# Every second row's mean of squares by statistics operations on VectorE, in a planned decoder-layer kernel on eight cores

## Chip, cores, metric
One Trainium2 chip, 8 cores, one launch. Every core computes 2048 of the 16384 positions. The time is the device time of the slowest core in microseconds (us). The engines are TensorE (PE), VectorE (DVE), ScalarE (ACT), GpSimd (POOL) and SyncE (SP).

## What is computed
One decoder layer, float32 in and out, width 1024. Cut to what matters here:

```
h = rms_norm(x, g_pre_mix)            # x / sqrt(mean(x*x) + 1e-6) * g, over the 1024 columns
proj = h @ w_in                       # q, k, v (768 each), pool input 256, gates 2048
q, k = rope(q), rope(k)
# attention in three head groups: (window, dilation) = (128,1), (512,4), (2048,16)
# multi-scale pooling branch, gated merge, output projection, norm, residual
x = x + rms_norm(merged @ w_out, g_post_mix)
gu = rms_norm(x, g_pre_ffn) @ w_gate_up
x = x + rms_norm((silu(a) * b) @ w_down, g_post_ffn)
```

The change is in the first `rms_norm` alone.

## The kernel before
A core reads its own 2048 rows (xo) and the 2048 rows ahead of them (xh, the halo, which the long attention windows need), each as 16 row blocks of 128 x 1024 float32. In the loop at line 896, 32 turns, blocks are taken in pairs. Both blocks of a pair get a sum of squares: the first (e = 0) by ScalarE's Square with an accumulator (L907), the second (e = 1) by a scalar_tensor_tensor of VectorE that multiplies the block with itself and accumulates (L905). ScalarE makes both into 1/sqrt with an Ln and an Exp over two columns (L909, L910). Then `to_feature_major` lets ScalarE copy the block, scaled, to bfloat16 (xsb, a ring of two), TensorE transpose it in eight pieces against ident, and VectorE copy the result from PSUM into hT (own rows) or hTh (halo). x blocks have eight buffers (xst), halo blocks five (xsth).

From hT and hTh come first the projections of the dilation-16 group: q2 and k2 per 512 rows (`qk2_unit`, through `rope`: two groups of eight 512-wide matmuls, four multiplications with the rotary table tab on VectorE into rt, a ring of two, and two additions on GpSimd), and v2 in 16 blocks per half (`v2_unit`, eight 256-wide matmuls each), every one of which reads all 16 row blocks of its half. The weights wq2, wk2, wv2 are loaded by GpSimd's queue and multiplied with the gains on VectorE (`gained`). Then the other two groups' projections (wq01, wk01, wv01), dilation-16 attention, and per 512 rows attention, pooling and merge; then output projection and the feed-forward part.

The order of the work isn't written out. The program records all operations as nodes; `schedule` simulates the five engines with the costs of `op_cost`, the priority of a node being its number plus a bias per part (table `PART`, L26), and what comes out is each engine's fixed order. Where TensorE would idle over 1 us in the simulation, `fill` (L356) puts matmuls on a constant tile warmw there. VectorE operations with two inputs in SBUF of more than one column and GpSimd operations exclude each other in the simulation (`port`, L153). Loads at the start wait for the load five before them (`behind`, FLIGHT); `WV_AT` (L24) says after how many x blocks the load of wv2 stands. Most operations bear line L522 or L524 in the profile, a helper's lines; tiles tell them apart.

Of the kernel before, what the change touches and what calls it, by code (L numbers as in the profile page):

```python
# [6 lines left out]
F32 = mybir.dt.float32  # L7
BF16 = mybir.dt.bfloat16
AF = mybir.ActivationFunctionType
ALU = mybir.AluOpType  # L10
# [3 lines left out]
D = 1024  # L14
# [4 lines left out]
EPS = 1e-6  # L19
# [1 line left out]

MERGE_AT = 1
FLIGHT = 5
WV_AT = 10  # L24

PART = {"norm": -615, "norm_h": -320, "qk2": 0, "k2h": -175, "v2": 650, "v2h": 15, "f-1": 90, "f0": 40, "f1": 0, "f2": 40, "f3": 0, "g2": -435,  # L26
        "a0": -100, "a1": 295, "a2": 0, "a3": -25, "p0": 0, "p1": 0, "p2": -15, "p3": 135, "m01": 0, "m23": 0, "w01": 0, "gv2": 275, "wg": 25}
ARENA_BASE = 18432
ARENA_BYTES = 229376 - ARENA_BASE

# [176 lines left out]
def peek(a):  # L207
    return a.resolve(0) if isinstance(a, View) else a


def in_psum(a):
    return type(peek(a).tensor).__name__.startswith("PSum")


def nelem(ap):
    n = 1
    for _, c in list(ap.ap)[1:]:
        n *= int(c)
    return n
# [6 lines left out]
def unit_step(ap):  # L226
    d = [x for x in list(ap.ap)[1:] if int(x[1]) > 1]
    return not d or int(d[-1][0]) in (0, 1)
# [5 lines left out]
def op_cost(eng, method, aps, kw):  # L234
    n = nelem(peek(aps[0]))
    if eng == "tensor":
        if method == "transpose":
            return 0.06
        rows = int(list(peek(aps[1]).ap)[0][1])
        return 0.013 + 0.00025 * n if rows <= 64 else max(n * 0.000422, 0.03)  # L240
    strided = not all(unit_step(peek(a)) for a in aps[1:])
    if eng == "scalar":
        n = max(n, nelem(peek(aps[1])))
        return 0.19 + 0.00086 * n + (0.19 if "accum_out" in kw else 0.0)
    if eng == "vector":
        if method == "reciprocal" or kw.get("op") == ALU.divide:
            return 0.1 + 0.00645 * n
        if all(peek(a).dtype == BF16 and not in_psum(a) for a in aps):
            return 0.12 + 0.00060 * n
        if method == "tensor_copy" and all(peek(a).dtype == BF16 for a in aps):  # L250
            return 0.14 + 0.00054 * n
        return 0.12 + 0.00110 * n
    if kw.get("op") == ALU.pow:
        return 0.55
    if method == "tensor_scalar":
        return 0.2 + 0.0026 * n
    return 0.17 + (0.0040 if strided else 0.0021 if unit_step(peek(aps[0])) else 0.0025) * n
# [316 lines left out]
def build_program():  # L574
# [30 lines left out]
    P = Prog(nc)  # L605
    pe, act, dve, pool, sp = P.pe, P.act, P.dve, P.pool, P.sp
# [14 lines left out]
    o = 0  # L621

    def take(nbytes):
        nonlocal o
        r = o
        o += (nbytes + 63) // 64 * 64
        return r


# [10 lines left out]
    nhalf = P.sb("nhalf", [128, 1], F32, take(4))  # L640
    uh = P.sb("uh", [128, 2, 16], F32, take(128))
    st = P.ring("st", [128, 2], F32, [take(8) for _ in range(16)], False)
    st4 = P.ring("st4", [128, 4], F32, [take(16) for _ in range(3)], False)
    R_HT = take(32 * KB)
    R1 = take(32 * KB)
# [15 lines left out]
    v2 = P.sb("v2", [128, 16, 2, 6, 64], BF16, R2 + 24 * KB)  # L661
# [7 lines left out]
    junk = P.ring("junk", [128, D], BF16, [R3 + 32 * KB + i * 2 * KB for i in range(2)], False)  # L669
# [32 lines left out]
    def x_load(i):  # L702
        src, ring = (xo, xst) if i < NT else (xh, xsth)
        j = i % NT
        t = ring.new()
        t.tok = sp.dma(t[:, :], src[j * 128:(j + 1) * 128, :], after=behind())
        loads.append(t.tok)
        sp_x.append(t.tok)
        return t
# [31 lines left out]
    def w2_load(w, src, got, todo, c, name):  # L741
        got.append(pool.dma(w[:, c, :, :], src[4 + c], dsem(name), after=behind()))
        loads.append(got[-1])
        todo.append((w[:, c, :, :], got[-1]))
# [5 lines left out]
    for c in range(2):  # L750
        w2_load(wk2, wk_d, d_wk2, g_wk2, c, "d_wk2_%d" % c)
    xt += [x_load(i) for i in range(4, WV_AT)]
    d_wv2 = pool.dma(wv2[:, :, :], wv_d[2], dsem("d_wv2"), after=behind())
    loads.append(d_wv2)
    xt += [x_load(i) for i in range(WV_AT, NT + 5)]

# [103 lines left out]
    gk_k2 = [gained(w, d, 128) for w, d in g_wk2]  # L860
    P.bias = PART["gv2"]
    gk_v2 = gained(wv2[:, :, :], d_wv2, 256)
# [33 lines left out]
    for i in range(2 * NT):  # L896
        halo = i >= NT
        P.bias = PART["norm_h" if halo else "norm"]
        if i % 2 == 0:
            pair = [xt.pop(0), xt.pop(0)]  # L900
            sums, sqs = st4.new(), []
            for e, u in enumerate(pair):
                src, j_ = u[:, :], junk.new()
                if e == 1:
                    sqs.append(dve.scalar_tensor_tensor(out=j_[:, :], in0=src, scalar=1.0, in1=src, op0=ALU.mult, op1=ALU.mult, accum_out=sums[:, e:e + 1], after=[u.tok]))  # L905
                else:
                    sqs.append(act.activation(out=j_[:, :], in_=src, func=AF.Square, accum_out=sums[:, e:e + 1], after=[u.tok]))  # L907
                j_.free(sqs[e])
            ln = act.activation(out=sums[:, 0:2], in_=sums[:, 0:2], func=AF.Ln, scale=1.0, bias=D * EPS, after=sqs)  # L909
            sums.tok = act.activation(out=sums[:, 2:4], in_=sums[:, 0:2], func=AF.Exp, scale=-0.5, after=[ln])  # L910
        t = pair[i % 2]
        j = (i % NT) * 128
        cp, h_ok[i] = to_feature_major(t[:, :], sums, any1, xsb.new(), None, (hTh if halo else hT)[:, :, j:j + 128], [],
                                       x_cp[:NT] if halo else [], col=2 + i % 2)
        t.free(cp)
        x_cp.append(cp)
        if halo and i + 5 < 2 * NT:
            xt.append(x_load(i + 5))
        if i % 4 == 3:
            s = (i // 4) % 4  # L920
            P.bias = PART["k2h" if halo else "qk2"]
            if not halo:
                qk2_unit("q", s, False)
            qk2_unit("k", s, halo)
        if i == NT - 1:
            P.bias = PART["v2"]
            for r in range(16):
                v2_unit(r, False)
            todo = [("k%d" % c, wk01[:, c, :, :], wk_d[c]) for c in range(4)] + [("v%d" % g, wv01[:, g, :, :], wv_d[g]) for g in range(2)]
            todo += [("u%d" % c, wu[:, c, :, :], wu_d[c]) for c in range(2)] + [("q%d" % c, wq01[:, c, :, :], wq_d[c]) for c in range(4)]  # L930
    P.bias = PART["w01"]
    d_masks = sp.dma(masks[:, :, :], masks_d[:, :, :], dsem("d_masks"), after=[sp_x[-1]])
# [4 lines left out]
    for g in range(4):  # L937
        c, hf = g // 2, g % 2
        d_mix.append(pool.dma(wmixb[64 * hf:64 * hf + 64, c, 64 * hf:64 * hf + 64], wmix_d[g, :, :], dsem("d_mix%d" % g), after=[sp_x[-1], m_mix]))
    P.bias = PART["v2h"]  # L940
    for r in range(16):
# [581 lines left out]
```

How the kernel before makes its waits and increments, by code:

```python
    def emit(self):  # L480
# [19 lines left out]
                if e.seen.get(proc, 0) >= val:  # L500
                    continue
                e.seen[proc] = val
                snap = self.procs[proc].snaps.get(val)
                if snap:
                    for k, v in snap.items():
                        if e.seen.get(k, 0) < v:
                            e.seen[k] = v
                s = self.procs[proc].sem
                e.meta.append(("wait", proc, val))
                e.ops.append(lambda q, s=s, val=val: q.wait_ge(s, val))
            sem, step = (sem, 16) if n.dma else (e.proc, 1)
            many = len(n.items) if n.dma else 1
            sem.count += step * many
# [6 lines left out]
                k = {q: res(x) for q, x in kw.items()}  # L520
                if n.dma or j == len(n.items) - 1:
                    e.ops.append(lambda q, m=method, a=a, k=k, s=sem.sem, v=step: getattr(q, m)(*a, **k).then_inc(s, v))
                else:
# [2 lines left out]
    def finish(self, last):  # L526
        e, need = self.sp, {}
        for n in last:
            need[n.tick[0]] = max(need.get(n.tick[0], 0), n.tick[1])
        for p, v in need.items():
            if e.seen.get(p, 0) < v:
                e.meta.append(("wait", p, v))
                e.ops.append(lambda q, s=self.procs[p].sem, v=v: q.wait_ge(s, v))
```

## Time and profile before

| | |
|---|---|
| median of 3 runs | 974.02 us (973.38 to 975.49) |
| profiled execution | 975.52 us, slowest core's span 972.5 us |
| spans of the eight cores | 964.8 to 972.5 us |
| TensorE busy | 937.4 us |
| VectorE busy | 473.3 us |
| ScalarE busy | 342.1 us |
| GpSimd busy | 353.9 us |
| granted TensorE clock, mean of the core | 0.986 |

The span is the time from the slowest core's first to its last instruction; the 3.0 us between it and the execution's own time lie around it. Busy times of engines overlap. A granted clock of 1 is 2.4 GHz.

### The profile page before, as it was taken

Reading aid. Unit: us, or ns where it says so; the run is one execution under the profiler, and the core shown is the slowest. Engines: PE = TensorE matmul, PEld = TensorE weight load, DVE = VectorE, ACT = ScalarE, POOL = GpSimd, SP = SyncE. Lnnn points to the kernel's source line nnn. Section 1 sums busy time; section 2 is a strip of 40 time slices with the busy share of each in tenths; the row PEclk is TensorE's granted clock in tenths of the full one; section 3 lists DMA queues with packets and bytes.
Section 4 is the critical chain, followed back from the end, with each engine's and each line's share of the span. In section 5 each row is a group of like instructions: output and inputs, shape, how many; then the busy total and the mean of one; then the engine's idle time right before and its main releaser. Section 6 shows DMA issues by size and latency. Waiting matters only on the chain.

```text
span 972.5 us, 15020 instructions; the slowest of 8 cores (964.8 to 972.5 us)
## 1 busy us (share of the span) xinstructions
PE 937.4 (96%) x5416; PEld 472.7 (49%) x5416; DVE 473.3 (49%) x560; ACT 342.1 (35%) x555; POOL 353.9 (36%) x334
## 2 busy tenths in 40 slices
PE   8879999989999999999999999999999999999997
PEld 3446776644554454444444444444444444444443
DVE  4889886686887867575454111111223111111323
ACT  4667426553445446434483111110101111110211
POOL 1447855467865584775693101110001000000000
PEclk8899999998999999999999999999999999999999
DMA  8936852451223477554377666563233545350221
GB/s 203 277 120 224 184 112 75 96 149 44 45 66 80 74 151 148 168 133 116 109 240 186 116 125 114 106 111 85 89 130 109 84 68 86 66 87 1 87 109 65
DMA packets 41224, 112.76 MB, mean 116 GB/s; under 512 B 5984, under 2 KB 14688, under 8 KB 41056
## 3 DMA queue, kind: packets, MB, share of 16 engines
q0 software_dynamic: 14432, 45.65, 27.7%
q1 hardware_dynamic: 26320, 66.07, 20.7%
q8 instruction: 44, 0.72, 0.3%
q14 instruction: 28, 0.23, 0.1%
q10 hardware_dynamic: 400, 0.08, 0.0%
HBM read 136.14 MB, written 21.30 MB: 162 GB/s over the span
## 4 chain that ended last, share of the span: by engine, by line
PE 84%; issue 4%; DVE 4%; DMA 3%; POOL 2%; ACT 2%; DVEq 0%; ACTq 0%; POOLq 0%; SPq 0%
PE ps L524 74%; PE ps L522 10%; DMA wq<-wq 1%; DMA wgs<-wg 1%; POOL x1b L522 1%; POOL st L522 1%; DVE junk L522 1%; ACT xsb L522 1%; DVE PT L522 1%; DMA tab<-tab 1%; DVE x1b L522 1%; DVE rt L522 0%; ACT junkd L522 0%; ACT xs L522 0%; DVE val L522 0%
## 5 line engine op out<-in xcount | busy, mean ns | idle before, releaser
L524 PE MATMUL ps<-hT,wgu 128*128 128x512 bf16 x1232 | 294.6, 379 | 0.0
L524 PEld LDWEIGHTS ps<-hT,wgu 128*128 128x128 bf16 x1232 | 120.4, 98 | 144.9
L522 DVE TENSOR_TENSOR ffT<-ps,sa 128x512 bf16<-128x512 f32 x88 | 60.8, 691 | 230.5 <-PE ps L522 226.4
L522 ACT ACTIVATE sa<-ps 128x512 f32<-128x512 f32 x88 | 52.4, 596 | 239.9 <-PE ps L522 239.9
L524 PE MATMUL ps<-wdna,ffT 128*128 128x512 bf16 x512 | 115.7, 379 | 1.0 <-issue 0.5
L522 POOL DMA_DIRECT2D wgu<-wgu x44 | 23.6, 537 | 245.8 <-PE ps L522 226.1
L524 PE MATMUL ps<-hT,wgs 128*128 128x512 bf16 x448 | 108.6, 383 | 3.1 <-ACT tg L522 2.1
L522 POOL TENSOR_TENSOR k<-rt 128x512 bf16<-128x512 f32 (+1 forms) x36 | 80.0, 2229 | 42.7 <-DVE rt L522 42.7
L522 DVE TENSOR_TENSOR rt<-ps,tab 128x512 f32<-128x512 f32 (+1 forms) x120 | 76.1, 669 | 20.2 <-PE ps L522 14.7
L522 ACT ACTIVATE junkd<-ps 128x1024 bf16<-128x1024 f32 (+1 forms) x33 | 32.8, 993 | 147.0 <-PE ps L522 147.0
L524 PEld LDWEIGHTS ps<-wdna,ffT 128*128 128x128 bf16 x512 | 50.0, 98 | 61.8 <-issue 1.9
L522 DVE TENSOR_TENSOR x1b<-ps,gfin 128x1024 f32<-128x1024 f32 (+1 forms) x17 | 19.8, 1162 | 116.4 <-ACT junkd L522 109.3
L524 PEld LDWEIGHTS ps<-hT,wgs 128*128 128x128 bf16 x448 | 43.1, 98 | 56.6 <-issue 8.0
L522 PE MATMUL ps<-hT,wgu 128*128 128x512 bf16 x176 | 66.7, 379 | 0.0
L522 DVE SCALAR_TENSOR_TENSOR tg<-tg,ps 128x512 f32<-128x512 f32 x64 | 43.2, 684 | 44.3 <-ACT tg L522 33.6
L522 DVE TENSOR_TENSOR PT<-PT,masks 128x1024 bf16<-128x1024 bf16 x48 | 54.9, 1148 | 18.4 <-ACT PT L522 18.2
L522 ACT ACTIVATE tg<-ps 128x512 f32<-128x512 f32 x64 | 38.1, 595 | 72.3 <-PE ps L522 72.2
L522 POOL TENSOR_TENSOR q<-rt 128x512 bf16<-128x512 f32 x24 | 49.8, 2084 | 37.7 <-DVE rt L522 37.7
L522 ACT ACTIVATE PT<-ps 128x1024 bf16<-128x1024 f32 x48 | 49.1, 1023 | 31.4 <-PE ps L522 31.2
L522 POOL TENSOR_TENSOR mT<-tg 128x512 bf16<-128x512 f32 x32 | 49.3, 1542 | 27.5 <-DVE tg L522 27.4
L524 PE MATMUL ps<-wout,mT 128*128 128x512 bf16 x224 | 53.6, 379 | 0.6 <-DVE tg L522 0.6
L522 DVE TENSOR_TENSOR wgs<-wgs,gains 128x2048 bf16<-128x2048 bf16 x16 | 44.2, 2766 | 4.6 <-DMA wgs<-wg 4.5
(149 smaller groups left out, 1308.3 us busy)
## 6 DMA issues: line engine op xcount, KB each, us to landing
wgu<-wgu POOLq DMA_DIRECT2D x44, 512.0 KB, 6.2
xst<-xo SPq DMA_DIRECT2D x16, 512.0 KB, 8.3
xsth<-xh SPq DMA_DIRECT2D x16, 512.0 KB, 6.1
wgs<-wg POOLq DMA_DIRECT2D x16, 512.0 KB, 6.0
xin<-xo SPq DMA_DIRECT2D x16, 512.0 KB, 5.9
x1s<-x1b SPq DMA_DIRECT2D x16, 512.0 KB, 4.4
xin<-x1s SPq DMA_DIRECT2D x16, 512.0 KB, 4.3
out<-x1b SPq DMA_DIRECT2D x15, 512.0 KB, 2.9
```

Of the source, the lines that this page charges most:

```text
L522: e.ops.append(lambda q, m=method, a=a, k=k, s=sem.sem, v=step: getattr(q, m)(*a, **k).then_inc(s, v))
L524: e.ops.append(lambda q, m=method, a=a, k=k: getattr(q, m)(*a, **k))
```

## The change
The second block of each pair gets its mean of squares from VectorE's statistics: two bn_stats of 512 columns, one bn_aggr that makes mean and variance of the two, and one scalar_tensor_tensor of one column, mean x mean + variance. The first block's Square is scaled by 1/32, so that both are means, and the Ln multiplies by 1024. VectorE writes no junk tile any more; there is a ring bns of three. `op_cost` knows bn_stats. `WV_AT` goes from 10 to 16, many entries of `PART` change, and `take` rounds to 32 bytes instead of 64.

```diff
-WV_AT = 10
+WV_AT = 16
-PART = {"norm": -615, "norm_h": -320, "qk2": 0, ...
+PART = {"norm": -790, "norm_h": -270, "qk2": -50, ...
...
+        if method == "bn_stats":
+            return 0.12 + 0.00110 * nelem(peek(aps[1]))
...
+    bns = P.ring("bns", [128, 14], F32, [take(56) for _ in range(3)], False)
...
-                src, j_ = u[:, :], junk.new()
+                src = u[:, :]
                 if e == 1:
-                    sqs.append(dve.scalar_tensor_tensor(out=j_[:, :], in0=src, scalar=1.0, in1=src, op0=ALU.mult, op1=ALU.mult, accum_out=sums[:, e:e + 1], after=[u.tok]))
+
+                    bn = bns.new()
+                    b6 = [dve.bn_stats(out=bn[:, 6 * h:6 * h + 6], in_=u[:, 512 * h:512 * h + 512], after=[u.tok]) for h in range(2)]
+                    ag = dve.bn_aggr(out=bn[:, 12:14], in_=bn[:, 0:12], after=b6)
+                    sqs.append(dve.scalar_tensor_tensor(out=sums[:, e:e + 1], in0=bn[:, 12:13], scalar=bn[:, 12:13], in1=bn[:, 13:14], op0=ALU.mult, op1=ALU.add, after=[ag]))
+                    bn.free(sqs[e])
                 else:
-                    sqs.append(act.activation(out=j_[:, :], in_=src, func=AF.Square, accum_out=sums[:, e:e + 1], after=[u.tok]))
-                j_.free(sqs[e])
-            ln = act.activation(out=sums[:, 0:2], in_=sums[:, 0:2], func=AF.Ln, scale=1.0, bias=D * EPS, after=sqs)
+                    j_ = junk.new()
+                    sqs.append(act.activation(out=j_[:, :], in_=src, func=AF.Square, scale=1.0 / 32.0, accum_out=sums[:, e:e + 1], after=[u.tok]))
+                    j_.free(sqs[e])
+            ln = act.activation(out=sums[:, 0:2], in_=sums[:, 0:2], func=AF.Ln, scale=float(D), bias=D * EPS, after=sqs)
```

What the planner makes of it differs in the start of the program; TensorE's order is the same in both from behind the dilation-16 attention on.

TensorE, from the first transposes (ident,xsb) on; warmw are filling matmuls. Before:

```order
L524 MATMUL ps<-ident_43,xsb_58_100 128x128 x7
L522 MATMUL ps<-ident_43,xsb_58_100 128x128
L524 MATMUL ps<-warmw_50 128x512 x8
L522 MATMUL ps<-warmw_50 128x512
L524 MATMUL ps<-ident_43,xsb_57_99 128x128 x7
L522 MATMUL ps<-ident_43,xsb_57_99 128x128
L524 MATMUL ps<-ident_43,xsb_58_100 128x128 x7
L522 MATMUL ps<-ident_43,xsb_58_100 128x128
L524 MATMUL ps<-warmw_50 128x512 x2
L522 MATMUL ps<-warmw_50 128x512
```

Now:

```order
L526 MATMUL ps<-ident_43,xsb_61_103 128x128 x7
L524 MATMUL ps<-ident_43,xsb_61_103 128x128
L526 MATMUL ps<-warmw_50 128x512 x2
L524 MATMUL ps<-warmw_50 128x512
L526 MATMUL ps<-ident_43,xsb_60_102 128x128 x7
L524 MATMUL ps<-ident_43,xsb_60_102 128x128
L526 MATMUL ps<-ident_43,xsb_61_103 128x128 x7
L524 MATMUL ps<-ident_43,xsb_61_103 128x128
L526 MATMUL ps<-terms_106,spread_107 128x512
```

Nine and three fills between these transposes and behind them have become three and none. Over the whole start there are 47 fills ahead of the first transposes and 35 behind before, 55 and 9 now.

TensorE, around the last halo transposes. Before, with v2 of the own half (wv,hT) ahead of them:

```order
L524 MATMUL ps<-wv_56_98,hT_73 128x256 x7
L522 MATMUL ps<-wv_56_98,hT_73 128x256
L524 MATMUL ps<-ident_43,xsb_57_99 128x128 x7
L522 MATMUL ps<-ident_43,xsb_57_99 128x128
L524 MATMUL ps<-ident_43,xsb_58_100 128x128 x7
L522 MATMUL ps<-ident_43,xsb_58_100 128x128
L524 MATMUL ps<-warmw_50 128x512 x2
L522 MATMUL ps<-warmw_50 128x512
L524 MATMUL ps<-hTh_74,wk_55_97 128x512 x7
```

Now:

```order
L526 MATMUL ps<-ident_43,xsb_60_102 128x128 x7
L524 MATMUL ps<-ident_43,xsb_60_102 128x128
L526 MATMUL ps<-ident_43,xsb_61_103 128x128 x7
L524 MATMUL ps<-ident_43,xsb_61_103 128x128
L526 MATMUL ps<-hT_76,wk_58_100 128x512 x7
L524 MATMUL ps<-hT_76,wk_58_100 128x512
L526 MATMUL ps<-hT_76,wk_58_100 128x512 x7
L524 MATMUL ps<-hT_76,wk_58_100 128x512
L526 MATMUL ps<-hTh_77,wk_58_100 128x512 x7
```

Ahead of the last transposes stand, beside fills and transposes, 184 matmuls of 512 columns and 128 of 256 before, 152 and 56 now; the rest has moved behind them.

VectorE, at the product of wv2 with the gains. Before:

```order
L522 SCALAR_TENSOR_TENSOR junk_59_101,st_28_70<-xst_42_84 128x1024
L522 COPY hT_73<-ps 128x8x128 x3
L522 TENSOR_TENSOR rt_70_112<-ps,tab_67_109 128x512 x2
L522 TENSOR_TENSOR wv_56_98<-wv_56_98,gains_46 128x2048
L522 COPY hT_73<-ps 128x8x128
```

Now:

```order
L524 BN_STATS bns_28_70<-xst_51_93 128x6 x2
L524 BN_AGGR bns_28_70<-bns_28_70 128x2
L524 SCALAR_TENSOR_TENSOR st_31_73<-bns_28_70 128x1
L524 TENSOR_TENSOR rt_72_114<-ps,tab_71_113 128x512
L524 TENSOR_TENSOR wv_59_101<-wv_59_101,gains_46 128x2048
L524 COPY hT_76<-ps 128x8x128 x2
```

Eight copies into hT stood ahead of it, now twelve, and the sums of all own rows. On GpSimd's queue the load of wv2 stood ahead of the first two rotary additions, now behind them.

## Rows read from the trace of the kernel before

**Rows 1.** The page: engine totals, then TensorE's granted clock in 40 slices.
```profile
PE 937.4 (96%) x5416; PEld 472.7 (49%) x5416; DVE 473.3 (49%) x560; ACT 342.1 (35%) x555; POOL 353.9 (36%) x334
...
PEclk8899999998999999999999999999999999999999
```

**Rows 2.** Stretches: length, busy PE, PEld, DVE, ACT, POOL, clock, DMA, GB/s.
```profile
13.70:67.70 54.00, 42.33 (x250) 21.50 (x248) 42.88 (x56) 33.85 (x55) 19.27 (x9) 0.84 0.73 203
67.70:111.70 44.00, 43.18 (x355) 30.82 (x355) 38.82 (x59) 32.05 (x60) 34.66 (x21) 1.00 0.66 208
```

**Rows 3.** Waits of TensorE before 120 us: total us, times, longest.
```profile
PE ps L524 <- ACT xsb L522: 5.0, 7, 3.0
```

**Rows 4.** Timeline of VectorE: start, length (us), operation.
```profile
13.72 1.22 DVE L522 SCALAR_TENSOR_TENSOR junk<-xst 128x1024 bf16<-128x1024 f32 x1
...
27.84 1.22 DVE L522 TENSOR_TENSOR wk<-wk,gains 128x1024 bf16<-128x1024 bf16 x1
28.97 1.88 DVE L522 TENSOR_TENSOR rt<-ps,tab 128x512 f32<-128x512 f32 x3
...
37.86 2.28 DVE L522 SCALAR_TENSOR_TENSOR junk<-xst 128x1024 bf16<-128x1024 f32 x1 [0.32 <-DMA xst<-xo]
...
59.18 1.88 DVE L522 COPY hT<-ps 128x1024 bf16<-128x1024 bf16 x3
60.97 1.21 DVE L522 SCALAR_TENSOR_TENSOR junk<-xsth 128x1024 bf16<-128x1024 f32 x1
...
62.12 1.28 DVE L522 TENSOR_TENSOR rt<-ps,tab 128x512 f32<-128x512 f32 x2
...
111.04 0.69 DVE L522 COPY hTh<-ps 128x1024 bf16<-128x1024 bf16 x1
```

**Rows 5.** Groups of VectorE, row sums: busy us, mean ns, idle before.
```profile
L522 DVE SCALAR_TENSOR_TENSOR junk<-xst 128x1024 bf16<-128x1024 f32 x8 | 16.5, 2078 | 1.4 <-DMA xst<-xo 1.4
L522 DVE SCALAR_TENSOR_TENSOR junk<-xsth 128x1024 bf16<-128x1024 f32 x8 | 13.2, 1658 | 0.0
```

**Rows 6.** Waits of VectorE from 13.7 to 111.7 us.
```profile
DVE hT L522 <- PE ps L522: 8.5, 7, 2.6
DVE hTh L522 <- PE ps L522: 3.5, 5, 1.2
```

**Rows 7.** Small operations of the pooling branch and the GpSimd addition beside one.
```profile
221.24 1.40 DVE L522 TENSOR_TENSOR uY<-uY,small 64x16 f32<-64x16 f32 x1
222.74 0.16 DVE L522 TENSOR_TENSOR zT<-uY,ps 64x16 bf16<-64x16 f32 x1
...
220.65 1.95 POOL L522 TENSOR_TENSOR q<-rt 128x512 bf16<-128x512 f32 x1
```

**Rows 8.** Timeline of TensorE.
```profile
16.97 0.91 PE L524 MATMUL ps<-ident,xsb 128*128 128x128 bf16 x7 [3.01 <-ACT xsb L522]
...
18.82 3.62 PE L524 MATMUL ps<-warmw 128*128 128x512 bf16 x8
...
22.66 0.72 PE L524 MATMUL ps<-ident,xsb 128*128 128x128 bf16 x7
...
107.74 0.93 PE L524 MATMUL ps<-wv,hT 128*128 128x256 bf16 x7
...
108.61 0.93 PE L524 MATMUL ps<-wv,hT 128*128 128x256 bf16 x7
...
111.88 1.67 PE L524 MATMUL ps<-hTh,wk 128*128 128x512 bf16 x7 [0.30 <-DVE hTh L522]
...
113.60 0.59 PE L524 MATMUL ps<-hTh,wk 128*128 128x512 bf16 x2
```

**Rows 9.** Timeline of ScalarE: Ln and Exp, then the two scaled copies.
```profile
107.40 0.49 ACT L522 ACTIVATE st<-st 128x2 f32<-128x2 f32 x2
107.99 2.19 ACT L522 ACTIVATE xsb<-xsth,st 128x1024 bf16<-128x1024 f32 x2
```

**Rows 10.** Loads of wv by GpSimd's queue: us to landing, of three.
```profile
DMA to landing us min/median/max: 10.4/15.3/16.9
```

More of the change, by code:

```diff
@@ L23 @@
 FLIGHT = 5
-WV_AT = 10
-PART = {"norm": -615, "norm_h": -320, "qk2": 0, "k2h": -175, "v2": 650, "v2h": 15, "f-1": 90, "f0": 40, "f1": 0, "f2": 40, "f3": 0, "g2": -435,
-        "a0": -100, "a1": 295, "a2": 0, "a3": -25, "p0": 0, "p1": 0, "p2": -15, "p3": 135, "m01": 0, "m23": 0, "w01": 0, "gv2": 275, "wg": 25}
+WV_AT = 16
+PART = {"norm": -790, "norm_h": -270, "qk2": -50, "k2h": -175, "v2": 575, "v2h": 0, "f-1": 0, "f0": 50, "f1": 0, "f2": 40, "f3": 0, "g2": -235,
+        "a0": -300, "a1": 270, "a2": 0, "a3": -25, "p0": 0, "p1": 0, "p2": -15, "p3": 135, "m01": 0, "m23": 10, "w01": -10, "gv2": -200, "wg": 0}
 ARENA_BASE = 18432
@@ L625, in take @@
         r = o
-        o += (nbytes + 63) // 64 * 64
+        o += (nbytes + 31) // 32 * 32
         return r
```

## The prediction, blind

> **What bounds the kernel now.** I read the page first: TensorE is busy for 96% of the span, and its granted clock is below full only at the beginning and in one slice near 210 us [rows 1]. So time can be won only where TensorE idles, runs filling matmuls, or runs at the low clock. The table of stretches shows where that is: from 13.7 to 67.7 us TensorE has a mean clock of 0.84 and gaps of 12 us, from 67.7 to 111.7 us it is nearly full at a clock of 1.00 [rows 2]. The list of waits says for whom it waits before 120 us: above all the normalised rows of ScalarE (xsb) [rows 3]. This is the chain that the change touches: row sums, Ln and Exp, scaled copy, transposes, copy into hT or hTh.
>
> The order of TensorE behind the first 143.7 us of its real work is the same in both programs, so I look only at the start. There, two points count. All own rows must be in hT before v2 of the own half can start, and the last halo rows must be transposed before TensorE can finish the halo.
>
> **VectorE's account before.** From 13.72 us, its first row sum, to 111.7 us, its last hTh copy [rows 4], VectorE has 98.0 us. Three multiplications with the rotary table last 1.88 us and two 1.28, so one takes 0.60 from start to start and ends 0.08 later; three copies take 1.79 up to the next instruction, a row sum 1.15, a weight multiplication of 1024 columns 1.13 [rows 4]. The sixteen row sums last 16.5 and 13.2 us [rows 5], where the shortest is 1.21: 16 x 1.22 = 19.5, so 10.2 us of the 29.7 are stretching, a mean of 0.64 for a row. Less 0.08 us each in which the next instruction has begun, they hold the engine for 28.4 us. With 44 rotary multiplications (26.4), 32 copies (19.2), three weight products of 1024 columns and one of 2048 (3.4 + 2.2) the sum is 79.6, and 18.4 us are idle, most of it for TensorE's transposes: 8.5 + 3.5 [rows 6], and 1.4 for x [rows 5].
>
> **The new row sum.** A bn_stats reads 512 columns, one source, nothing from PSUM; no such instruction is in the trace. Nearest is the rotary multiplication of 512 columns, 0.60 from start to start; the two halves have no wait between them, 1.20. Then a dependent bn_aggr and a dependent one-column product. Nearest to those are the small operations of the pooling branch, 0.16 us, which start 0.10 us after the one before has ended [rows 7]. 1.20 + 0.08 + (0.10 + 0.17) + (0.10 + 0.17) - 0.08 = 1.74, I take 1.75. Bounds: 1.4, if most of a gap is covered by a neighbour (the planner puts copies between the halves), and 2.4, if a statistics operation passes its data at two thirds of that rate. So in itself the new form costs VectorE 0.6 us more for a row, 9.6 us for sixteen.
>
> **The stretching.** The last product still has two inputs in SBUF (mean and variance), like the old one. A product of 64x16 that began at 221.24 us lasted 1.40 us, where its neighbour of the same size took 0.16, and ended at 222.64, when GpSimd's addition of 220.65 + 1.95 ended [rows 7]. So size does not protect: it will wait for a running GpSimd addition. But GpSimd starts when a rotary pair is done, the old sum came right behind such pairs and took the whole 2 us, and now 1.5 us of statistics run first. GpSimd is busy for 54 of these 98 us [rows 2], so at random a product would meet 0.55 x 1.0 us, 8.8 in all; the eight old stretchings less 1.5 us each leave 0.9. I take 4 us. ScalarE's side only gets scale=1/32 and scale=1024 in instructions that are there anyway: nothing. The junk buffer that VectorE no longer writes leaves both to ScalarE; its squares come earlier, which costs nothing, since it idles 20 us before 67.7 [rows 2].
>
> The Trainium skill (VectorE: DVE Perf Modes, The TRN2 errata) gives (N + 151) / 0.96 ns for an fp32 tensor_tensor, 0.69 us at 512. The trace has that as the duration (0.69 for one) but 0.60 as the pitch; with 0.69 for each half, as an estimate, the set would be 0.18 us dearer, 2.9 us over sixteen, and the whole sum 0.2 us slower than before instead of faster.
>
> **The new order.** Four moves count.
> First, fills. Behind the first transposes the old order has 35 filling matmuls, nine of them from 18.82 to 22.66 us, at the low clock of 1.2 GHz, 0.43 each, right ahead of transposes that then started without a wait [rows 8]. The new one has 9. The first block grows from 47 to 55; at 0.216 it ends 1.7 us later than 13.96 (16.97 less 3.01), still ahead of the first transposes at 16.97 [rows 8], which themselves wait 0.4 us more for the longer row sum.
> Second, the load of wv2 goes behind x row 15, on POOL behind two additions. x rows 10 to 15 land earlier, their sums stand earlier on VectorE. Its product with the gains now waits for a load that is issued only when row 11 has landed; loads of wv took 10.4 to 16.9 us [rows 10]. Before, VectorE still had to wait for row 9 at 37.86 [rows 4]; with 1 MB less ahead of it row 11 may land near 39, and wv2 from 49 to 54 us. VectorE is there at 13.7 + 8 sets 14.0 + stretching 2 + 9 rotary multiplications 5.4 + 12 copies 7.2 + products 3.4 + idle 4 = 49.7. So it costs from 0 to 5 us, with the copies of rows 12 and 13 queued behind it. I take 0, since the other two wv loads followed four others in the queue, and make the rest a rival.
> Third, less is asked before the last transposes. TensorE then has done 32 wide and 72 narrow matmuls fewer: 32 x 0.215 + 72 x 0.109 = 14.7 us (eight wide in 1.72 us, eight narrow in 0.87 [rows 8]), and VectorE has 32 rotary multiplications instead of 44 ahead of its last hTh copy, 30 ahead of its last row sum. They stand behind.
> Fourth, the memset of v01 stands ahead of the last two hTh copies, 2.3 us; TensorE has other work there (40 wide matmuls, 8.6 us), so nothing; if that cover were gone it would cost those 2.3.
>
> **The sum.** TensorE takes up the halo's last part at 111.88 us [rows 8]. With 14.7 us less behind it, break-even for that point is 97.2. VectorE's new account up to the last row sum: 16 x 1.75 = 28.0, stretching 4, 30 rotary multiplications 18.0, 28 copies 16.8, products 5.6, together 72.4, from 13.7 to 86.1 plus idle. Then Ln and Exp 0.6, two scaled copies 2.2 [rows 9], transposes 0.5: 89.4 plus idle. Idle: x 1.4 [rows 5] and the first transposes 1.2 stay, the longest wait, 2.6 before [rows 6], falls to about 1 with fewer fills, and 1.5 is left of the rest because TensorE has 27 us of work in 36 instead of 42 in 44. That is 5.1, so 94.5, and 97.2 - 94.5 = **2.7 us faster**. The profiled execution took 975.5, the median is 974.0; from the median 971.3.
>
> **Rivals.**
> A, slower: the one-column product meets a GpSimd addition as often as the long one did. Place: VectorE behind each pair of statistics, with ScalarE's Ln and the row's transposes behind it. At the old mean of 0.64 us that is 10.2 us instead of 4: 97.2 - 100.7, 3.5 us slower, 977.5. It turns the sign above 0.42 us a row. For it: the 1.40 us. Against: what GpSimd waits for is done 1.5 us before. The Trainium skill (SBUF — State Buffer, Who interferes with whom) has the rule that a VectorE instruction with two SBUF inputs contends with a GpSimd instruction that reads SBUF; by that rule, the trace agrees with its 1.40 us.
> B, slower: wv2 lands 5 us after VectorE wants it, the late end above: 97.2 - 99.5, 2.3 slower, 976.3; it turns the sign above 2.7 us.
> C, no change: in the halo half ScalarE is the pace. It is busy 32 of 44 us there [rows 2] and would have to do nearly that in 36; five row buffers refill in 6 us. If this half takes 38.7 us instead of 36, 974.0.
> D, no change: the set costs 2.0 us instead of 1.75, because the halves do not overlap as the rotary multiplications do [rows 4] and the aggregate is dearer than the small operations [rows 7]: 4 us more, 1.3 slower, 975.3. The Trainium skill's formula named above lies near this case; the pitch of 0.60 in the trace speaks against it.
> E, much faster: stretching falls to 0.9 us as in the subtraction above. 3.1 more, 5.8 in all, 968.2.
>
> **Numbers.** Forecast 0.37, E 0.14, C 0.14, D 0.10, A 0.13, B 0.12. A difference of 0.2%, 2 us, is about what a measurement of this kernel can tell. Of the forecast 0.05 falls inside it. Faster 0.32 + 0.14 = 0.46, same 0.05 + 0.14 + 0.10 = 0.29, slower 0.13 + 0.12 = 0.25. The range goes from 1.7 below E, 966.5, to A's centre, 977.5; beyond lie half of A and the tail of E, some 0.12.
>
> **What would show it.** Right: bn_stats near 0.68 long and 0.60 apart, sixteen last products with a median under 0.3 and a sum under 7 us, last transposes before 96 us, clock over 0.9 between 40 and 60 us, GpSimd's additions down from 2.4 to 2.0 us. Wrong: one-column products of 1 to 2 us in most sets, a wait for DMA at wv's product, or TensorE waits between 65 and 95 us of more than 11 us.

## The result, and the profile after

The changed kernel took 997.56 us, median of 4 runs (995.61 to 1000.01); the kernel before took 974.02, 973.38 and 975.49 beside it. The ratio is 1.0238, 95% interval 1.0210 to 1.0265: slower by 2.4%. Forecast were 971.3 us, and a range that ended at 977.5. The ratios, and all medians but this first one, leave out executions in which a die was slower than the other at a lower mean clock, and none of which has a trace: 998.37 us among the four above, 1142.69 us beside it, later 1021.71 us of the changed kernel (mean clocks of 0.926 to 0.944 on cores 0 to 3) and 1137.70 us of the kernel before (0.818 to 0.837 on cores 4 to 7).

The result is made of two things of different kinds, a clock and the schedule, and they have to be taken apart first. The spans of the eight cores do it. View: span and mean granted clock of each core, changed kernel.

```profile
core 0: 994.4 us, clock 0.961
core 1: 991.2 us, clock 0.958
core 2: 994.4 us, clock 0.962
core 3: 994.1 us, clock 0.962
core 4: 972.8 us, clock 0.991
core 5: 977.2 us, clock 0.987
core 6: 998.5 us, clock 0.957
core 7: 998.1 us, clock 0.960
```

Six cores are some 20 us longer than the other two, at a mean clock of 0.96 instead of 0.99. Where that is, the stretches of the slowest core and of a fast one show. View: stretches of core 6, then of core 5: length, busy TensorE and its matmuls, granted clock, share of DMA, GB/s.

```profile
46.00:206.00 160.00, 150.03 (x1183) 0.81 0.49 122
206.00:400.00 194.00, 182.37 (x1215) 0.98 0.48 92
```

```profile
46.00:206.00 160.00, 145.73 (x1361) 0.99 0.55 137
206.00:400.00 194.00, 183.06 (x1139) 0.97 0.44 94
```

For 160 us core 6 has a granted clock of 0.81. That is neither of the two levels of [rows 1] and [rows 2] (1.00, which is 2.4 GHz, and half of it): a third one, 0.8125 in the records. TensorE is busy in it and gets fewer matmuls done. View: groups of TensorE's instructions from 120 to 200 us: busy us, mean ns of one, idle before; core 6, then core 5.

```profile
L526 PE MATMUL ps<-hT,wq 128*128 128x512 bf16 x42 | 12.1, 437 | 0.0
```

```profile
L526 PE MATMUL ps<-hT,wq 128*128 128x512 bf16 x56 | 13.4, 380 | 0.0
```

The same matmul lasts 437 ns instead of 380. The level begins at 46.3 to 48.1 us and ends at 206 to 209 us on cores 0, 1, 2, 3, 6 and 7, with stretches of 3.4 us at half clock in it on four of them, and never comes on 4 and 5. The other three runs have no trace, but their spans and mean clocks (0.96 instead of 0.99) are alike: all eight cores are at 991.8 to 994.0 us, or all but cores 0 and 1 (976.2 and 975.2), or all but 2 and 3 (974.8 and 976.4). So cores are spared in pairs. No trace of the kernel before has the level, though TensorE is as busy there.

The Trainium skill (TensorE: Matmul & The Clock Gate, Part 1) names a limiter of 13/16 of the clock, which comes for a whole die once three of its cores run dense matmuls, and holds as long as the load does. The size agrees with the 0.8125. The rest does not, in the traces: the kernel before is as dense on all eight cores without it (96.6 to 98.7 of 100 us busy, from 100 to 200 us, at a clock of 1.00), here two cores of a die went free, and it ended near 207 us while the load went on (182 of the next 194 us busy).

**Without that clock** the changed kernel is still slower. Cores 4 and 5 above say so, and later runs of the same program on three chips (which chip the first timing had is not recorded), with no 0.81 in their three traces: 981.74 us (8 runs, ratio to before 1.0059, interval 1.0040 to 1.0079), 981.04 and 981.47, and 981.16. So some 6 to 7 us of the 23.5 belong to the change's own schedule (5.7 by the ratio, 7.1 by the medians), and some 16 to 17 to the clock. The rest of this section reads core 5, which had the full clock.

View: core 5, groups of VectorE from 13.7 to 97.9 us, just behind the end of its last row sum: busy us, mean ns, idle before. They answer to [rows 5].

```profile
L524 DVE TENSOR_TENSOR rt<-ps,tab 128x512 f32<-128x512 f32 x31 | 20.2, 682 | 2.9 <-PE ps L524 2.6 <-issue 0.3
L524 DVE COPY hT<-ps 128x1024 bf16<-128x1024 bf16 x16 | 10.6, 685 | 3.7 <-PE ps L524 3.6
L524 DVE BATCH_NORM_STATS2 bns<-xst 128x6 f32<-128x512 f32 x16 | 10.4, 681 | 0.0
L524 DVE BATCH_NORM_STATS2 bns<-xsth 128x6 f32<-128x512 f32 x16 | 10.2, 679 | 0.0
L524 DVE COPY hTh<-ps 128x1024 bf16<-128x1024 bf16 x12 | 7.9, 684 | 2.1 <-PE ps L524 1.9
L524 DVE SCALAR_TENSOR_TENSOR st<-bns 128x1 f32<-128x1 f32 x16 | 7.7, 483 | 1.7
L524 DVE BATCH_NORM_AGGREGATE bns<-bns 128x2 f32<-128x12 f32 x16 | 3.3, 206 | 1.2
```

A bn_stats of 512 columns lasts 0.68 us, an aggregate 0.21. The one-column products last 0.483 in the mean; one instruction's view of them (shortest, median, longest in ns) says why.

```profile
L524 DVE SCALAR_TENSOR_TENSOR st<-bns x16: 219/221/1893, 15.6 to 96.0; 128x1 f32<-128x1 f32 x16
```

Most last 0.22, a few up to 1.89. View: timeline of VectorE, then of GpSimd and of ScalarE, around the last of them.

```profile
93.27 0.68 DVE L524 TENSOR_TENSOR rt<-ps,tab 128x512 f32<-128x512 f32 x1
93.87 1.27 DVE L524 BATCH_NORM_STATS2 bns<-xsth 128x6 f32<-128x512 f32 x2
95.07 0.67 DVE L524 TENSOR_TENSOR rt<-ps,tab 128x512 f32<-128x512 f32 x1
95.66 0.19 DVE L524 BATCH_NORM_AGGREGATE bns<-bns 128x2 f32<-128x12 f32 x1
95.95 1.89 DVE L524 SCALAR_TENSOR_TENSOR st<-bns 128x1 f32<-128x1 f32 x1
97.77 0.68 DVE L524 TENSOR_TENSOR rt<-ps,tab 128x512 f32<-128x512 f32 x1
```

```profile
95.88 1.94 POOL L524 TENSOR_TENSOR k<-rt 128x512 bf16<-128x512 f32 x1 [0.18 <-DVE bns L524]
```

```profile
97.94 0.50 ACT L524 ACTIVATE st<-st 128x2 f32<-128x2 f32 x2 [1.45 <-DVE st L524]
98.58 2.19 ACT L524 ACTIVATE xsb<-xsth,st 128x1024 bf16<-128x1024 f32 x2
```

The product of one column begins at 95.95 and ends at 97.84, when GpSimd's addition (95.88 + 1.94 = 97.82) ends; ScalarE's Ln has waited 1.45 us for it. And behind Ln and the copies the last halo rows wait. View: TensorE from 92.7 us.

```profile
92.71 0.93 PE L526 MATMUL ps<-wv,hT 128*128 128x256 bf16 x7
93.47 0.27 PE L524 MATMUL ps<-wv,hT 128*128 128x256 bf16 x1
95.98 0.55 PE L526 MATMUL ps<-ident,xsb 128*128 128x128 bf16 x7 [2.24 <-DVE bns L524]
...
99.88 0.55 PE L526 MATMUL ps<-ident,xsb 128*128 128x128 bf16 x7 [1.11 <-ACT xsb L524]
100.26 0.22 PE L524 MATMUL ps<-ident,xsb 128*128 128x128 bf16 x1
100.92 0.55 PE L526 MATMUL ps<-ident,xsb 128*128 128x128 bf16 x7 [0.43 <-ACT xsb L524]
101.30 0.22 PE L524 MATMUL ps<-ident,xsb 128*128 128x128 bf16 x1
101.36 1.67 PE L526 MATMUL ps<-hT,wk 128*128 128x512 bf16 x7
```

TensorE is through with the last transposes and goes on at 101.36 us, with a group of the own half (hT,wk) that the new order has put there. Forecast for this point were 94.5, break-even 97.2: 4.2 us late, and the core ends 4.7 us later than the core of [rows 8] (977.2 against 972.5).

### The profile page after: what moved, and what is told of

It reads as the page before. It is cut to its first block, busy times and chain, and to the rows that moved or that the text cites. A ratio compares the mean times of both kernels' runs of the same rounds, so it can differ in the third digit from the quotient of the medians.

```text
span 998.5 us, 15099 instructions; the slowest of 8 cores (972.8 to 998.5 us)
## 1 busy us (share of the span) xinstructions
PE 957.4 (96%) x5398; PEld 483.3 (48%) x5398; DVE 475.1 (48%) x592; ACT 343.3 (34%) x555; POOL 343.2 (34%) x334
## 4 chain that ended last, share of the span: by engine, by line
PE 88%; DVE 4%; issue 3%; DMA 2%; ACT 2%; POOL 1%; DVEq 0%; ACTq 0%; POOLq 0%
PE ps L526 77%; PE ps L524 10%; DMA wgs<-wg 1%; DMA wq<-wq 1%; DVE bns L524 1%; ACT xsb L524 1%; DVE rt L524 1%; DVE st L524 1%; DVE hT L524 0%; POOL st L524 0%; DVE val L524 0%; DVE PT L524 0%; DVE wgs L524 0%; DVE den L524 0%; DVE hTh L524 0%
## 5 line engine op out<-in xcount | busy, mean ns | idle before, releaser
L524 POOL TENSOR_TENSOR k<-rt 128x512 bf16<-128x512 f32 (+1 forms) x36 | 71.8, 2005 | 50.7 <-DVE rt L524 50.6
L524 DVE TENSOR_TENSOR x1b<-ps,gfin 128x1024 f32<-128x1024 f32 (+1 forms) x17 | 19.8, 1162 | 116.4 <-ACT junkd L524 116.4
L524 POOL TENSOR_TENSOR mT<-tg 128x512 bf16<-128x512 f32 x32 | 48.1, 1507 | 29.6 <-DVE tg L524 29.5
L526 PE MATMUL ps<-wv,hT 128*128 128x256 bf16 x336 | 48.8, 293 | 2.0 <-DVE hTh L524 1.7
```

Of the source, the lines that this page charges most:

```text
L524: e.ops.append(lambda q, m=method, a=a, k=k, s=sem.sem, v=step: getattr(q, m)(*a, **k).then_inc(s, v))
L526: e.ops.append(lambda q, m=method, a=a, k=k: getattr(q, m)(*a, **k))
```

## Experiments

An order of instructions is kept exactly in most of these kernels: the planner runs as before, and only then are single instructions exchanged. "L" is the start of the last matmul of the halo transposes (101.30 above), mean over the eight cores of the profiled execution. It is 108.8 us before and 100.6 in the changed kernel (`after_again`). Other executions of the same program gave 101.2 and 101.5, so a difference in L of about 1 us says nothing by itself.

### Is it the order or the operations?

`order_products`: after the planner has run, each set gives way to one product (the edit is shortened here, as are those below).

```diff
-bn_stats(bn[0:6], u[0:512]); bn_stats(bn[6:12], u[512:1024]); bn_aggr(bn[12:14], bn[0:12])
-scalar_tensor_tensor(sums, mean, mean, var, mult, add)
+scalar_tensor_tensor(scratch, u, 1/1024, u, mult, mult, accum_out=sums)
```

> The changed kernel's order of instructions on every engine, instruction for instruction, but each of the 16 sets of statistics operations is again one product of the row with itself (scaled by 1/1024, so that all sums keep the changed kernel's meaning); the whole row is read in one instruction of about 1.2 us instead of a set of about 1.75 us. Theory A (the gap in TensorE's work near 34-37 us and what follows it sets off the granted clock of 0.81, whatever VectorE does): the 0.81 stage of about 160 us appears on most cores, the time is 990 to 1000 us. Theory B (the statistics operations themselves set it off): no core shows 0.81, the time is 973 to 981 us. The 8 us in which the changed kernel's undisturbed cores are later than before would stay under theory 'order' and shrink by 3 or more under theory 'sets'.

Measured: 979.77 and 980.29 us, ratio 1.0059 (1.0039 to 1.0079), L 99.9, no 0.81. Taken alone this speaks for theory B. It was run again beside the changed kernel:

> The changed kernel itself, once more. Four executions of it had the granted clock of 0.81 on six or eight cores for about 160 us from 46 to 48 us on, and took 995.6 to 1000.0 us; the kernel with its order but with products (980 us) and the one with 14 fills (979 us) had none, in a session of their own. Theory A' (what sets 0.81 off is in the changed kernel: its gap and its sets together): 0.81 again, 995 to 1000 us, and again not beside it in the kernel with products. Theory D (0.81 belongs to the chip or the session in which the changed kernel was first timed): no 0.81 here, 975 to 981 us.

> The changed kernel's order with products in place of the statistics sets, once more, beside the changed kernel itself. Theory A': no 0.81, 979 to 981 us, while the changed kernel has it. Theory D: both without it or both with it.

Measured on one chip: changed kernel 981.74 us, 1.0059 (1.0040 to 1.0079), L 100.6, no 0.81 anywhere; with products 978.72, 1.0046 (1.0031 to 1.0061), L 99.2. Neither A nor B is left as a sufficient cause of 0.81: the changed kernel itself does without it. Nor is the wait near 34 us, as this view of it on core 3 of `after_again` shows.

```profile
37.73 0.91 PE L526 MATMUL ps<-ident,xsb 128*128 128x128 bf16 x7 [3.70 <-ACT xsb L524]
```

That is the same wait, as long as in the first timing, and the clock was 1.00 or 0.50 all the way behind it. What the pair shows for the change: with products, too, the order costs 4 to 6 us. The sets seem to cost some 1 to 3 us more in it, but the two intervals overlap. As work on VectorE they cost much more than that: the sixteen products hold it for 23 to 27 us on the eight cores of `order_products` (24.7 to 27.9 busy, less 16 x 0.08), the sets for 33.5 (16 x 1.83 and 4.2 of stretching).

`stats_old_order`: the sets in the order of before.

> The kernel before with its own order on every engine, instruction for instruction, but each of VectorE's 16 products in the first 112 us is a set of two bn_stats, a bn_aggr and a one-column product at the same place. Theory A (the order's gap and fills set off the granted clock of 0.81): no 0.81 stage, and the time is that of before plus or minus what the sets cost: 972 to 980 us. Theory B (statistics operations set it off): 0.81 for about 160 us on most cores, 990 to 1000 us.

Measured: 975.87 us, ratio 1.0020 (1.0009 to 1.0031), L 110.8, no 0.81. The sets alone cost 2 us here (by the ratio), although their one-column products are hardly stretched in this order (median 220 ns, longest 1040, 5.3 us in sum instead of 7.1 to 8.3).

### The fills

`after_with_fills` has 14 filling matmuls ahead of the transposes of row 4; `before_no_fills` is the kernel before with `del fills[1].items[3:]` and `order.remove(fills[3])`.

> The changed kernel with 14 filling matmuls of 512 columns ahead of the transposes of row 4, where TensorE waits 3.7 us for ScalarE near 34 us; nothing else moves. Theory A (TensorE's rest near 34-37 us, which lets the granted clock fall to 0.5 and rise again in one step at the same time on all cores, sets off 0.81): no 0.81 stage, 974 to 982 us. Theory B (statistics operations) and theory C (the denser ScalarE and DMA work at 40 to 60 us): 0.81 stays, 990 to 1000 us.

> The kernel before with the filling matmuls of the changed kernel: 3 instead of 9 ahead of the transposes of row 2, and none instead of 9 ahead of those of row 4; nothing else moves. Theory A (the rest near 34 us): a 0.81 stage appears on some cores, and the time goes to 985 to 1000 us. Theories B and C: no 0.81 stage, 973 to 977 us (the fills only cover a wait).

Measured: with fills 978.53 and 979.57 us, L 99.9; before without them 975.43 us, 1.0015 (1.0005 to 1.0025), L 110.0, no 0.81 in either. So the fills of the kernel before are worth 1.5 us, which my sum had at nothing; and a wait near 36 us (1.65 us on its slowest core, not 3.7) did not bring the low level. As tests of theories A and B all runs of this chip are weak, since the changed kernel itself was not timed there and later did without the level too.

### The form of the last operation

```diff
-scalar_tensor_tensor(out=sums, in0=mean, scalar=mean, in1=var, op0=mult, op1=add)
+tensor_scalar(out=sums, in0=mean, scalar1=mean, scalar2=var, op0=mult, op1=add)
```

> The changed kernel with the one-column product (mean times mean plus variance) written as a tensor_scalar with two scalars read from memory, so that it has one tensor input from SBUF instead of two; nothing else moves. Theory 'GpSimd stretches two-input operations alone': its 16 executions fall from 8.0 us in sum (longest 2.2) to about 3.5 us (longest 0.3), the wait of 3.7 us near 34 us shrinks by 1 to 1.5 us, and the undisturbed cores end 0.5 to 2 us earlier. Theory 'any one-column operation behind the sums waits as long': no difference. On 0.81: theory A' says it stays if the wait of TensorE near 34 us stays over 2.5 us; theory D that it goes as in the changed kernel beside it.

> The kernel before with its own order and the sets of statistics operations, the last operation of each in the form of a tensor_scalar. With the two-input form it took 975.9 us against 974.4 of before (ratio 1.0020). If the stretched one-column products were what it cost: 974.0 to 974.8 us, ratio within 0.1% of 1. If the longer set itself costs it: 975.5 to 976.2 us. No 0.81 by theory A' and by D alike unless before shows it.

View: the same instruction in `scalar_form`, core 5.

```profile
L524 DVE TENSOR_SCALAR st<-bns x16: 272/272/275, 15.0 to 92.6; 128x1 f32<-128x1 f32 x16
```

The stretching is gone, on all cores: 4.4 us in sum instead of 7.1 to 8.3, the longest 0.275. In the changed kernel's order this gives 977.53 us beside 981.74, ratio 1.0027 (1.0013 to 1.0041) instead of 1.0059, L 97.6 instead of 100.6. That is more than I expected, and about all that the instructions save (3.5 us), since the stretched ones stood where ScalarE waited. In the old order: 976.75 us, 1.0012 (0.9998 to 1.0026), no difference that shows, and L is 111.7, no earlier than with the stretched form (110.8). The Trainium skill (SBUF — State Buffer, Who interferes with whom) has contention for a VectorE instruction with two inputs in SBUF beside a GpSimd one; these runs agree with it, down to one column, and show that a second scalar from memory doesn't count as an input in that sense.

`scalar_and_fills` has both edits, `scalar_wv10` the scalar form and `WV_AT = 10`, planned anew.

> The changed kernel with the one-column product in the scalar form and with the 14 fills ahead of the transposes of row 4. Alone the scalar form gave 977.0 us (median of its undisturbed executions, changed kernel 981.7 beside it) and the fills 978.5 and 979.6. If the two gains are of different things (stretched operations between 80 and 100 us; the wait and the low clock near 34 to 43 us): 974 to 976 us, last halo transposes at 95 to 97 us. If the fills only cover a wait whose end does not move: 976.5 to 977.5 us, as with the scalar form alone.

> The changed kernel with the scalar form and with the load of wv2 behind x row 9 again, as before the change, its order planned with that; the start of v2 products can come earlier, x rows 10 to 15 land later. If the late load of wv2 is what thins TensorE's work between 80 and 100 us: 974 to 975.5 us. If VectorE's own queue sets the last halo transposes, as its account of the changed kernel says (busy for 86% until its last row sum): 976 to 978.5 us.

Measured: 978.83 us, 1.0044 (1.0027 to 1.0060), L 98.3: the fills add nothing to the scalar form, and the time lies above both expectations. With wv2's load where it was before: 985.14 us, 1.0112 (1.0097 to 1.0127), L 101.8. Taking back that part of the change makes it worse in the new table of numbers. That the late load was not the fault is likely but not shown by this run alone, since the planner also moved other work. Both expectations of mine for it failed.

### What VectorE's work is worth

Half of the statistics left out: only the first 512 columns of each second row are read, in both orders.

```diff
-bn_stats(bn[6:12], u[512:1024])
-bn_aggr(bn[12:14], bn[0:12])
+bn_aggr(bn[12:14], bn[0:6])
```

> The changed kernel's order with the scalar form, but statistics of the first 512 columns of each second row only, so that half of each of the 16 sets' reading (16 x 0.6 = 9.6 us of VectorE's work) is left out. Theory V (VectorE's work plus a fixed idle time gives the last halo transposes): they come 8 to 9 us earlier than in scalar_form (95.1 to 98 us on most cores), near 88 to 90, and the time falls from 977.5 to 969 to 971 us. Theory W (the chain row sum, ScalarE, transposes and copies with its own waits sets them, and work taken from VectorE turns into idle time): they come 1 to 4 us earlier, 93 to 96, and the time is 973.5 to 976.5 us.

> The order of before with the scalar form, but statistics of the first 512 columns only. Theory V: last halo transposes 8 us earlier than with full sets (109 to 114 us), 101 to 106, and 967 to 969 us. Theory W: 106 to 111, 972.5 to 974.5 us.

Measured: new order 972.08 us, 0.9982 (0.9972 to 0.9992), L 92.9, 4.7 earlier than `scalar_form`; old order 970.32 us, 0.9963 (0.9949 to 0.9976), L 103.4, 8.3 earlier than `scalar_form_old_order`. Of 9.6 us of work, half (new) to nearly all (old) reaches the last transposes, and 4.4 to 4.8 us the time (from the ratios, times 974). By L that is theory V in the old order and between V and W in the new one; both times lie between the two theories.

The computation is not whole in these two kernels. But they point to a lever: not another kind of sum on VectorE, but fewer sums on VectorE. In the kernel before, 3 or 5 of the 16 products are moved to ScalarE, with the whole computation and all else in place.

```diff
+for k in (2, 4, 6):          # five_on_scalar: (2, 4, 6, 9, 12)
+    n.eng = P.act
+    n.items = [activation(out=junk, in_=u, func=Square, accum_out=sums[:, 1])]
```

> The kernel before, with 3 of VectorE's 16 products (the third, fifth and seventh) as a Square with a sum on ScalarE right behind its neighbour's, and all else in its place. VectorE has 3 x 1.8 = 5.5 us less, stretching included, ScalarE 3 x 1.25 = 3.7 us more in a stretch in which it idles 10 of 28 us. Theory V (VectorE's work counts to half or more, as with half statistics: 4.4 to 4.8 us of time for 9.6 us of work): 2.6 us faster than before, 971 to 972.5 us. Theory S (ScalarE's chain of two squares, Ln, Exp and two copies gets longer for these pairs and takes it back): 973.5 to 976 us.

> The same with 5 of the 16 (the tenth and the thirteenth as well, which are of halo rows). Theory V: 4 us faster than before, 969.5 to 971.5 us. Theory S: slower than with three, since ScalarE is busy for 14.3 of 18 us between 68 and 86 us, 973 to 977 us.

Measured: three: **969.69 us**, ratio 0.9947 (0.9934 to 0.9959), L 104.5. Five: 973.85 us, 0.9985 (0.9976 to 0.9994), L 106.8. With three it beats both kernels, and by twice what I had expected. View: groups of VectorE in `three_on_scalar`, core 2, which answer to [rows 5]: busy us, mean ns, idle before.

```profile
L522 DVE SCALAR_TENSOR_TENSOR junk<-xsth 128x1024 bf16<-128x1024 f32 x8 | 13.3, 1663 | 0.0
L522 DVE SCALAR_TENSOR_TENSOR junk<-xst 128x1024 bf16<-128x1024 f32 x5 | 6.4, 1278 | 1.6 <-DMA xst<-xo 0.8 <-ACT st L522 0.7
```

The own rows' sums cost VectorE 6.4 us instead of 16.5: three are gone, which were stretched ones (2.06, 2.28 and 2.98 us before), and the five that are left last 1.28 in the mean, where the same five took 1.86: only one of them (1.51) is still above 1.22. Five are worse than three: TensorE's waits for xsb are 11.0 us on the slowest core, against 7.6 with three and 5.0 in [rows 3]; the halo rows' copies stand behind ScalarE's longer queue, as theory S has it (argued from this, not tried by itself).

### Does 0.81 come back?

> The changed kernel itself, a third time. At its first timing: a granted clock of 0.81 for 160 us on six to eight cores, 995.6 to 1000.0 us. At its second: none, 978.4 to 983.9 us. Theory D (the 0.81 belongs to the chip of the first timing, as something that this kernel's start can set off there): either of the two again, with all executions alike. Theory E (it comes and goes with the single execution, by chance): executions of both kinds side by side.

> The changed kernel itself. Theory D (0.81 belongs to the chip of the first timing): none on chips 6, 7 and 9 so far; on a chip that has it, every execution takes 995 to 1000 us with 0.81 on at least six cores, on any other 979 to 983 us. Theory E (it comes by chance with the single execution): about one execution in four would show it, and none of eleven did outside the first timing.

> The changed kernel's order with products in place of the sets. If the changed kernel beside it shows 0.81: with theory A (the order and its wait near 34 us bring it) this one shows it too, 992 to 998 us; with theory B (the statistics operations bring it) it doesn't, 978 to 981 us. If the changed kernel doesn't show it: 978 to 981 us by both.

> The order of before with the statistics sets. If the changed kernel beside it shows 0.81: with theory B this one shows it too, 990 to 996 us; with theory A it doesn't, 975 to 977 us. If the changed kernel doesn't show it: 975 to 977 us by both.

Measured: changed kernel 981.04 and 981.47 us on one chip (ratio 1.0072, 1.0052 to 1.0092), 981.16 on another; beside the latter the order with products 980.51, the sets in the old order 976.79 (one run). None of the 19 traces of these experiments and the kernel before has a granted clock other than 1.00 or 0.50.

That does not clear the kernel before of the level, nor does it rule out theory E. The later executions without it are eleven that had the full mean clock on every core; two more of the changed kernel (1021.71 and 1010.12 us) had mean clocks of 0.926 to 0.955 on one die. An estimate: 160 us at 0.8125 take 0.03 off a core's mean, as between cores 5 and 6 above (0.987 and 0.957), so 180 to 340 us of it would give these means, and nearly the whole run would give the 0.818 to 0.837 of the kernel before in the 1137.70 us execution. No core of any execution on record has a mean below 0.811. So it may well be one and the same level, which comes in single executions whatever the kernel, and what is peculiar to the first timing is that it came in 4 of 4, on both dies, and for nearly the same time. No trace of such an execution was kept that could settle it. Theory D, that it belongs to the chip of the first timing, fits as well and isn't shown either. For which part of the change the level comes could not be tried, since no further trace showed it. **This stays open.**

## Why the prediction was wrong

**The clock.** The sum had only two levels of the clock, as the trace of before shows them, and took for granted that behind the start a busy TensorE has the full one. A third level for 160 us has no step in it, in no rival either. It made some 16 of the 26 us by which the forecast missed. What it costs can be read: core 6 reaches the matmul that is the 4000th from the end at 209.1 us, core 5 at 189.6, 19.5 us apart, and from there both need nearly the same time (789.4 and 787.6). Five cores with the level reach it at 208.4 us in the mean, six of `after_again` at 189.8. Its cause is not shown.

**The break-even was right.** The step "With 14.7 us less behind it" means 14.7 us less of TensorE's work done by then, and as much more still to do. It can be checked on every core that has all its records: from L to that same 4000th matmul from the end pass 74.4 to 74.5 us before (cores 1 to 5 and 7) and 88.3 to 89.6, mean 89.1, in `after_again` (cores 0, 1, 3, 5, 6, 7). That is 14.6 us more. So a kernel in the new order must have L 14.6 us earlier than 108.8 to be as fast as before, one in the old order no earlier. This turns L into a forecast of the time. All kernels timed on that footing agree with it within 1.8 us, where L itself repeats within 1.3 us:

| kernel | order | L, us | forecast from L | measured, from the ratio |
|---|---|---|---|---|
| changed, without 0.81 | new | 100.6 | +6.4 | +5.7 |
| the same, after_third | new | 101.2 | +7.0 | +7.0 |
| after_with_fills | new | 99.9 | +5.7 | +4.7 (two runs, from the medians) |
| order_products | new | 99.9 | +5.7 | +5.7 |
| order_products_2 | new | 99.2 | +5.0 | +4.5 |
| order_kept | new | 100.3 | +6.1 | +5.2 |
| scalar_form | new | 97.6 | +3.4 | +2.6 |
| scalar_and_fills | new | 98.3 | +4.1 | +4.3 |
| half_stats_new | new | 92.9 | -1.3 | -1.8 |
| stats_old_order | old | 110.8 | +2.0 | +1.9 |
| sets_kept | old | 109.5 | +0.7 | +2.4 (one run, from the medians) |
| scalar_form_old_order | old | 111.7 | +2.9 | +1.2 |
| before_no_fills | old | 110.0 | +1.2 | +1.5 |
| half_stats_old | old | 103.4 | -5.4 | -3.6 |
| three_on_scalar | old | 104.5 | -4.3 | -5.2 |
| five_on_scalar | old | 106.8 | -2.0 | -1.5 |

`scalar_wv10` has an order of its own, with 91.8 us from L to the 4000th matmul; with this its 101.8 gives +10.3, measured +10.9.

**The step that failed is VectorE's idle time**, "that is 5.1". The work up to the last row sum was forecast as 72.4 us with the gaps inside the sets. On core 5, the one for which this was read, it is 71.9 us busy and 2.9 of such gaps (1.7 and 1.2 in the groups above), 74.8. View: that stretch, then VectorE's waits in it.

```profile
13.70:97.90 84.20, 71.92 (x128) 0.92 0.71 213
```

```profile
DVE hT L524 <- PE ps L524: 3.6, 6, 1.1
...
DVE rt L524 <- PE ps L524: 2.6, 1, 2.6
DVE hTh L524 <- PE ps L524: 1.9, 3, 1.0
DVE wk L524 <- DMA wk<-wk: 0.7, 1, 0.7
DVE rt L524 <- issue: 0.3, 1, 0.3
```

These are 9.1 us where 5.1 stood: 8.1 of them for TensorE, for which I had 3.7 (1.4 more were for x, which it never had to wait for). I let the waits shrink with TensorE's work, and with fewer fills. But a wait for transposes is a round trip (sum, Ln and Exp, two copies, transposes, copy), and with less other work ahead of it the engine stands at it sooner. Two pairs of runs bear this reading out: in `half_stats_new` about half of the 9.6 us of work taken away came back as idle time (from 13.7 to 98 us VectorE idles 16.1 and 19.8 us on two of its cores, 12.2 on core 5 of `scalar_form`), and `order_products`, with 7 to 10 us less work on VectorE than the changed kernel, ends at most 3 us earlier.

The other terms by size: a set has a pitch of 1.83 us (13.91 to 15.74), I took 1.75: 1.3 us over sixteen. Stretching, 4.0 forecast, is 7.7 us on this core less 16 x 0.22, so 4.2 (4.5 where the sum is 8.0). The 30 rotary multiplications were counted rightly (the 31st of the group above begins at 97.77 us, behind the last product). The rest is about 1 us for the twelve waits, since an instruction that has waited lacks the 0.08 of overlap that the pitches count on. Together these are, within some tenths, the 2.4 us from 72.4 to 74.8, and with the 4.0 of idle time they make 6.4 of the 6.6 us by which the last row sum ended late (97.84 against 86.1 + 5.1).

**The parts one by one.** bn_stats at 0.68 and a pitch of 0.60, one-column products with a median of 0.22, and GpSimd's additions of k at 1.98 instead of 2.38 us: as forecast. The sum of the one-column products was to be under 7 us and is 7.1 to 8.3. Stretching of 4 us: right in size, and so rival A as priced (10.2 us) did not happen. But its mechanism is there, and taking it away gave 3.1 us (ratio 1.0059 to 1.0027): it was priced in, and sat on the path. Rival B: no wait for DMA at wv's product (it follows at 53.49 us without a gap), and the old load place was worse. Rival C: ScalarE was not the pace; from 67.7 to 101.7 us it is busy for 25.0 of 34 us, VectorE for 30.8. Rival D came to a third of its price: a set costs 1.83 us, not 2.0, which is 1.3 us of its 4. The fills, at nothing in the sum, are worth 1.5 us in the kernel before. The clock "over 0.9 between 40 and 60 us": 1.00 and 0.91 on cores 4 and 5, 0.80 to 0.85 on the other six. The slice of low clock that I read near 210 us in [rows 1] lies at 217.6 to 224.4 us, and a stretch of 3.4 us at 374.6 hides in a digit of 9; nothing rests on either. Last transposes "before 96": 98.5 and 101.3 on the two full-clock cores. TensorE's waits "more than 11 us between 65 and 95" were to show it wrong; on core 5 they are 2.9 (1.4 + 0.8 + 0.7). So this sign was badly chosen: the waits lie at 95.98 and 99.88 us and ahead of 65, and only the point at 97.2 decided.

## What to carry to other kernels

When a stage is a chain that passes through several engines, its length isn't the busiest engine's work plus some idle time: less work ahead of a round trip gives longer waits, and the account must follow the round trips, or fix a marker (here the last transposes) and ask when it comes in either order. Before a cheaper-looking operation is put on the engine that is fullest, try to move work off it: three row sums given to an engine that had room brought 5.2 us, another kind of sum for all sixteen cost 1.9 in the same order. And look at every core's span and clock before explaining a difference: of the 23.5 us here some 16 came with a clock for which no run here shows a cause. A run that lacks such a level says something of its cause only beside one that has it, on the same chip.

## What was not expected of the hardware

A third granted clock of 0.8125 that comes within 2 us on six cores (46.3 to 48.1 us), stays for some 160 us under a busy TensorE, ends with TensorE as busy as before, and spares cores in pairs, two of them on a die whose other two have it. By spans and mean clocks it was there in 4 of 4 runs of the first timing; eleven later ones of the same program have the full clock, two have a lower mean on one die and no trace. Matmuls of 512 columns last 437 instead of 380 ns in it, of 256 columns 306 instead of 274.

A VectorE product of one column with two inputs in SBUF can last 1.9 to 2.5 us beside a GpSimd addition (0.22 alone); the same arithmetic with one input and two scalars from memory lasts 0.272 every time.
